# Expert rows of a product-key layer gathered as u and v halves in two phases, with 32-column products for the v sum

## What is computed

```python
def block(hb):                     # 128 tokens at a time
    ...                            # scores, two top-16 lists per head, the best 16 of their 256 sums
    idx = jnp.take_along_axis(cand_i, pos, axis=-1)            # (128 tokens, 8 heads, 16)
    gate = jax.nn.softmax(top_s, axis=-1).astype(hb.dtype)
    u = expert_u[idx]
    act = jax.nn.gelu(jnp.einsum('thkd,td->thk', u, hb), approximate=False)
    vv = expert_v[idx]
    return jnp.einsum('thk,thkd->td', gate * act, vv)
```

## Time and profile before

| | us |
|---|---|
| three runs | 3162.23, 3163.95, 3174.32 |
| median | 3163.95 |
| the profiled execution, span | 3168.1 |
| the expert stage, from `peer_clear` (948.4) to the first addition to `X` of tile 3 (2344.4) | 1396.0 |

### The profile page before, as it was taken

One profiled execution on the slowest core, in us unless ns is written; L12 is line 12 of the kernel. 1 busy time (PEld: TensorE's weight loads), 2 busy tenths in 40 slices (PEclk: granted clock), 3 DMA queues, 4 the chain that ended last, 5 costly groups with the idle time before them and its releaser, 6 DMA issues. The chain is left out here.

```text
span 3168.1 us, 23012 instructions
## 1 busy us (share of the span) xinstructions
PE 2617.8 (83%) x7588; PEld 1312.0 (41%) x7588; DVE 1722.4 (54%) x3834; ACT 320.4 (10%) x765; POOL 582.0 (18%) x516
## 2 busy tenths in 40 slices
PE   6799399889997777867777777787789978999998
PEld 4455399844452233322323323333334433444443
DVE  3644865432077677576676677555535647333304
ACT  1123121010010000100001000100010010111100
POOL 0000000000003434434434444344410000000000
PEclk9899599689998888889889898899889988999999
DMA  3201000032189999989999999999942121122210
GB/s 117 93 7 54 0 1 1 1 139 80 64 296 384 379 379 395 380 364 385 390 387 367 380 373 387 379 393 410 417 179 80 60 105 68 53 80 80 80 67 27
DMA packets 126790, 655.73 MB, mean 207 GB/s; under 512 B 9456, under 2 KB 12144, under 8 KB 60912
## 3 DMA queue, kind: packets, MB, share of 16 engines
q0 software_dynamic: 73728, 536.90, 41.9%
q1 hardware_dynamic: 52976, 117.74, 10.3%
HBM read 652.51 MB, written 2.10 MB: 207 GB/s over the span
## 5 line engine op out<-in xcount | busy, mean ns | idle before, releaser
L705 PE MATMUL PD<-AR,C 128*128 128x512 f32 x2048 | 1027.9, 661 | 349.2 <-DVE C L1511 348.9
L1654 POOL DMA_INDIRECT AR<-in_uv,C x512 | 581.8, 1136 | 1740.7 <-DVE C L1452 926.5
L1503 DVE CUSTOM_DVE_ANT_0 AR<-AR,HN 128x1024 f32<-128x1024 f32 x512 | 620.2, 1225 | 426.3 <-DMA AR<-in_uv,C 420.3
L705 PEld LDWEIGHTS PD<-AR,C 128*128 128x128 f32 x2048 | 423.7, 212 | 953.4 <-issue 494.7
L435 PE MATMUL PA<-HT,WR 128*128 128x512 f32 x736 | 327.2, 604 | 3.0 <-ACT HT L810 2.1
L435 PE MATMUL PA<-AR,WR 128*128 128x512 f32 (+1 forms) x720 | 314.1, 605 | 6.4 <-ACT AR L881 4.9
L435 PEld LDWEIGHTS PA<-HT,WR 128*128 128x128 f32 x736 | 141.9, 194 | 179.1 <-issue 175.3
L435 PEld LDWEIGHTS PA<-AR,WR 128*128 128x128 f32 (+1 forms) x720 | 138.5, 194 | 181.6 <-issue 178.7
L979 ACT ACTIVATE SC<-SC 128x2 f32<-128x2 f32 x256 | 51.9, 204 | 1276.4 <-DVE SC L1503 1276.4
L1511 DVE TENSOR_SCALAR C<-C,SC 128x128 f32<-128x128 f32 x512 | 148.6, 349 | 1.6 <-ACT SC L979 1.6
L1621 DVE TENSOR_SCALAR HT<-HN,V 128x512 f32<-128x512 f32 x44 | 24.0, 546 | 198.2 <-ACT HN L1008 198.2
(11 more groups left out here) (322 smaller groups left out, 2274.4 us busy)
## 6 DMA issues: line engine op xcount, KB each, us to landing
WR<-in_w_ada SPq DMA_DIRECT2D x12, 2048.0 KB, 7.8
WR<-in_w_in SPq DMA_DIRECT2D x11, 2048.0 KB, 7.7
WR<-in_w_up SPq DMA_DIRECT2D x11, 2048.0 KB, 7.9
WR<-in_w_down SPq DMA_DIRECT2D x5, 2048.0 KB, 7.8
WR<-in_w_pq SPq DMA_DIRECT2D x4, 2048.0 KB, 8.0
AR<-in_uv,C POOLq DMA_INDIRECT x512, 9.4
WR<-in_w_o SPq DMA_DIRECT2D x2, 2048.0 KB, 7.9
WR<-in_w_out SPq DMA_DIRECT2D x2, 2048.0 KB, 7.7
```

The source lines that it names most:

```text
L705: ins = nc.tensor.matmul(acc[half], DG[:, j, :], UV[:, j, D + 512 * half:D + 512 * half + 512], start=False, stop=False)
L1503: ttr(UV[:, j, 0:D], UV[:, j, 0:D], HN[:, t, :], 1.0, 0.0, ALU.mult, ALU.add, DOT[:, g, j % GRP:j % GRP + 1]).then_inc(s["dots"], 1)
L1654: nc.gpsimd.indirect_dma_start(UV[:, turn % RING, :], None, uv, bass.IndirectOffsetOnAxis(ap=IDX[:, t % 2, i:i + 1], axis=0),).then_inc(uv ...
```

## The change

A gathered row is now 4 KB, and the ring `ROWS` has 16 slots of 4 KB instead of 8 of 8 KB, in the same memory. A tile has two phases of 128 gathers.

In the **u phase** gather k fetches, for each token (partition), the u row of its selection k. VectorE forms 128 sums into `DOTS`. Then ScalarE does one gelu over the 128 x 128 matrix, VectorE multiplies it by the gates, TensorE transposes it, and VectorE copies it to `WT`: now a partition is a selection and a column a token.

In the **v phase** a gather fetches, for one token, the v rows of its 128 selections, one to a partition. The indices for it are the transposed index matrix `IDXT`. Four tokens q, q + 32, q + 64, q + 96 make a quad. VectorE writes for each quad four 128 x 32 matrices that are zero but for column q, which holds the token's weights (line 1502 of the changed kernel, 8 slots ahead of TensorE). TensorE multiplies each with its token's row in two halves; the four products of a half go to four different groups of 32 output partitions. The number of 512-column products stays 256 a tile, and the zero products go. `select` for the next tile now runs in the v phase, a step ahead of every fourth quad, and `layer_rows` at the end of the tile.

```diff
-RING = 8
-GRP = 2
+RING = 16
+QUADS = P // 4
+WSLOTS = 8
@@ views of the shared tile AR
-        UV = AR[:, 0:RING * 2048].rearrange("p (r n) -> p r n", r=RING)
+        ROWS = AR[:, 0:RING * D].rearrange("p (r n) -> p r n", r=RING)
+        DOTS = ar(22528, NSEL)
+        WT = ar(22656, P)
-        DG = lvl[:, 0:1024].rearrange("p (r n) -> p r n", r=RING)
+        WQ = lvl[:, 0:1024].rearrange("p (r j n) -> p r j n", r=WSLOTS, j=4)
@@ TensorE
-                acc = [bank("d"), bank("d")]
-                for half in range(2):
-                    nc.tensor.matmul(acc[half], cc("zero")[0:1, :], fours, start=True, stop=False)
-                for first, last in ((0, TURN_AT), (TURN_AT, TURNS)):
-                    if first > 0 and t > 0:
-                        turn_block("xn3", t - 1, "aa")
-                    with pe.Fori(first, last) as it:
-                        for j in range(RING):
-                            pe.wait_ge(s["diag"], it * RING + (NSEL * t + j + 1))
-                            for half in range(2):
-                                ins = nc.tensor.matmul(acc[half], DG[:, j, :],
-                                                       UV[:, j, D + 512 * half:D + 512 * half + 512],
-                                                       start=False, stop=False)
-                            ins.then_inc(s["uv_used"], 1)
-                for half in range(2):
-                    full("d", nc.tensor.matmul(acc[half], cc("zero")[0:1, :], fours, start=False,
-                                               stop=True))
+                pe.wait_ge(s["idx"], t + 1)
+                transposes("d", [SS[t][:, 0:NSEL]])
+                if t > 0:
+                    turn_block("xn3", t - 1, "aa")
+                pe.wait_ge(s["wtok"], t + 1)
+                transposes("d", [DOTS])
+                acc = [bank("d"), bank("d")]
+                for q in range(QUADS):
+                    pe.wait_ge(s["wquad"], QUADS * t + q + 1)
+                    for half in range(2):
+                        for j in range(4):
+                            i = 2 * NSEL * t + NSEL + 4 * q + j
+                            if half == 0:
+                                pe.wait_ge(row_full[i % RING], 16 * (i // RING + 1))
+                            ins = nc.tensor.matmul(acc[half][32 * j:32 * j + 32, :], WQ[:, q % WSLOTS, j, :],
+                                                   ROWS[:, i % RING, 512 * half:512 * half + 512],
+                                                   start=(q == 0), stop=(q == QUADS - 1))
+                        if q == QUADS - 1:
+                            full("d", ins)
+                    if q < QUADS - 1:
+                        ins.then_inc(s["v_used"], 1)
+                pe.drain().then_inc(s["v_used"], 1)
@@ ScalarE
                 gate_exp(t)
-                for first, last in ((0, NORM_AT), (NORM_AT, TURN_AT), (TURN_AT, TURNS)):
-                    if first == NORM_AT and t > 0:
-                        roots(ffv(t - 1))
-                    if first == TURN_AT and t > 0:
-                        turned_both(t - 1)
-                    with act.Fori(first, last) as it:
-                        for g in range(RING // GRP):
-                            act.wait_ge(s["dots"], it * RING + (NSEL * t + GRP * (g + 1)))
-                            A(GEL[:, g, :], DOT[:, g, :], ACT.Gelu).then_inc(s["gelu"], 1)
+                if t > 0:
+                    turned_both(t - 1)
+                act.wait_ge(s["u_used"], NSEL * (t + 1))
+                tell(A(DOTS, DOTS, ACT.Gelu), "gelud")
+                roots(ffv(t))
@@ VectorE (select, step 7, then the loop over tiles)
-                    link(nc.vector.tensor_copy(IDX[:, t % 2, :], acc_[0]), "idx")
+                    link(ts(IDX[:, t % 2, :], acc_[0], 2.0, None, ALU.mult), "idx")
+                b = take()
+                link(ts(IDXT, b[:, 0:P], 2.0, 1.0, ALU.mult, ALU.add), "d_free")
+                tell(dve.nop(), "idxt")
                 gates(t)
...
+                for k in range(NSEL):
+                    i = 2 * NSEL * t + k
+                    row = ROWS[:, i % RING, :]
+                    dve.wait_ge(row_full[i % RING], 16 * (i // RING + 1))
+                    tell(ttr(row, row, HN[:, t, :], 1.0, 0.0, ALU.mult, ALU.add, DOTS[:, k:k + 1]), "u_used")
+                dve.wait_ge(s["gelud"], t + 1)
+                tell(tt(DOTS, DOTS, GATE[:, t % 2, :], ALU.mult), "wtok")
+                b = take()
+                link(nc.vector.tensor_copy(WT, b[:, 0:P]), "d_free")
+                by_quad = WT.rearrange("p (j q) -> p j q", j=4)
+                for q in range(QUADS):
+                    if q % 4 == 0 and t + 1 < NT:
+                        select(t + 1, q // 4)
+                    if QUADS * t + q >= WSLOTS:
+                        dve.wait_ge(s["v_used"], QUADS * t + q - WSLOTS + 1)
+                    tell(stt(WQ[:, q % WSLOTS, :, :], cc("iota").unsqueeze(1).broadcast_to([P, 4, 32]), float(q),
+                             by_quad[:, :, q:q + 1].broadcast_to([P, 4, 32]), ALU.is_equal, ALU.mult), "wquad")
                 for half in range(2):
                     b = take()
                     xs = X[:, t, 512 * half:512 * half + 512]
                     link(tt(xs, xs, b, ALU.add), "d_free")
-            layer_rows("xn3", NT - 1, X[:, NT - 1, :], HN[:, NT - 1, :])
+                layer_rows("xn3", t, X[:, t, :], HN[:, t, :])
@@ GpSimd
+            rows = uv.rearrange("e (h d) -> (e h) d", h=2)
+            def gather(i, index):
+                if i == RING // 2:
+                    pool.wait_ge(s["peer_clear"], 1)
+                if i >= RING:
+                    half, r = divmod(i - RING, NSEL)
+                    if half % 2 == 0:
+                        pool.wait_ge(s["u_used"], NSEL * (half // 2) + r + 1)
+                    else:
+                        pool.wait_ge(s["v_used"], QUADS * (half // 2) + r // 4 + 1)
+                nc.gpsimd.indirect_dma_start(
+                    ROWS[:, i % RING, :], None, rows, bass.IndirectOffsetOnAxis(ap=index, axis=0),
+                ).then_inc(row_full[i % RING], 16)
             for t in range(NT):
                 pool.wait_ge(s["idx"], t + 1)
...
+                for k in range(NSEL):
+                    gather(2 * NSEL * t + k, IDX[:, t % 2, k:k + 1])
+                pool.wait_ge(s["idxt"], t + 1)
+                for r in range(P):
+                    token = 32 * (r % 4) + r // 4
+                    gather(2 * NSEL * t + NSEL + r, IDXT[:, token:token + 1])
```

More of the change, by code:

```diff
@@ L153, in constants @@
     put("invfreq", (np.float32(10000.0) ** (-np.arange(HALF, dtype=np.float32) / np.float32(HALF)))[None, :])
-    put("iota", np.arange(TOPK)[None, :])
+    put("iota", np.arange(32)[None, :])
     cnt = [1.0 / np.minimum(np.arange(16) + 1, w) for w in POOL]
@@ L204, in build @@
                  "ct", "x1t", "tmid", "ycomb",
-                 "topk", "idx", "dots", "geluv", "diag", "uv_used", "csil",
+                 "topk", "idx", "idxt", "u_used", "geluv", "gelud", "wtok", "wquad", "v_used", "csil",
                  "bufs", "conv", "convsq", "silu_in", "silu", "pooled", "merged",
@@ L212, in build @@
         w_sem = [ctx.enter_context(nc.semaphore(f"w_slot{i}")) for i in range(NWR)]
-        uv_full = [ctx.enter_context(nc.semaphore(f"uv_full{i}")) for i in range(RING)]
+        row_full = [ctx.enter_context(nc.semaphore(f"row_full{i}")) for i in range(RING)]
         n = {nm: 0 for nm in names}
@@ L1443, in select @@
                     link(tt(eq, tpv.unsqueeze(2).broadcast_to([P, NSEL, TOPK]),
[L1444 removed]
+                            cc("iota")[:, 0:TOPK].unsqueeze(1).broadcast_to([P, NSEL, TOPK]), ALU.is_equal))
                     for h in range(H):
@@ L1488, in _ @@
             for t in range(NT):
+                b = take()
+                link(ts(IDXT, b[:, 0:P], 2.0, 1.0, ALU.mult, ALU.add), "d_free")
+                tell(dve.nop(), "idxt")
                 gates(t)
-                cuts = (0, NORM_AT) + (SELECT_AT if t + 1 < NT else ()) + (TURNS,)
-                for first, last in zip(cuts[:-1], cuts[1:]):
-                    if first == NORM_AT and t > 0:
-                        layer_rows("xn3", t - 1, X[:, t - 1, :], HN[:, t - 1, :])
-                    if first in SELECT_AT:
-                        select(t + 1, SELECT_AT.index(first))
-                    with dve.Fori(first, last) as it:
-                        for g in range(RING // GRP + 1):
-                            if g < RING // GRP:
-                                for j in range(GRP * g, GRP * g + GRP):
-                                    dve.wait_ge(uv_full[j], it * 16 + 16 * (NSEL // RING * t + 1))
-                                    ttr(UV[:, j, 0:D], UV[:, j, 0:D], HN[:, t, :], 1.0, 0.0, ALU.mult, ALU.add,
-                                        DOT[:, g, j % GRP:j % GRP + 1]).then_inc(s["dots"], 1)
-                            if g >= 1:
```

(5 more changed lines are left out.)

25 lines of the change are left out of this document (3 added, 22 removed), and 2 rows, old and new, of the table JOBS.

## The result

| | before | after |
|---|---|---|
| median of four runs each | 3163.1 us (3160.5 to 3174.3) | 3287.6 us (3275.7 to 3299.3) |
| ratio to before, 95% interval | | 1.040 (1.036 to 1.044) |
| span of the profiled execution | 3168.1 us | 3273.7 us |
| rows' stage, 948.4 us to the first addition to `X` of tile 3 | 1396 us | 1504 us |

The change made the kernel 4.0% slower; 3125 us, 1.2% faster, was forecast. The stage was to take 1356 us and takes 1504. What follows the stage is as long as before (821 us against 824), so all of the loss lies in the stage.

What follows compares the result with a forecast made beforehand. Transfers were taken to bound the rows' stage: from 948.4, 3.9 us to the first new row, 1015 gathers x 1.32 = 1340, three dry spells x 3 = 9, last quad 3.5; 39.6 us less, so 3125 us, range 3085 to 3330.

Steps and rivals of the forecast that it cites:

- Where the gain could come from: Rows' stage: about 16 us a tile to win in three tiles, and some 9 us at each end of a tile.
- The transfers, a pitch of 1.32 us: DMA queues: a half gather costs 1.282 to 1.351 us, middle 1.32 taken; short rows bring no gain.
- Rival 2: DMA queues: half gathers carry a price of their own, pitch 1.42 us, 3226 us in all; chance 0.09.
- GpSimd, a pitch of 1.24 us: Issue of gathers: 0.94 us each with 0.30 us between, under the transfers' 1.32, as products don't stretch them.
- Rival 3: GpSimd binds: gathers keep their mean of 1.136 us, pitch 1.44 us, 3247 us in all; chance 0.05.
- VectorE, 1.15 us: u phase: products start 1.15 us apart, so 147 us a phase lies under the transfers' 169 us.
- TensorE in the v phase: Column groups overlap in pairs: 3.5 us a quad, bounds 6.9 and 1.7, under 5.3 us for its four gathers.
- Rival 1: TensorE binds the v phase, column groups not overlapping: quad 6.9 us, 3322 us in all; chance 0.24.
- The seams: Between phases: u to v leaves the engines dry about 3 us, TensorE starting some 14 us late; v to u costs nothing.
- The sum: Stage's end: terms add to 2304.8 where 2344.4 us stood, 39.6 us less, giving 3125 us for the kernel.

Runs made afterwards that it cites:

- run 6: The kernel before, with its selection for the next tile cut into 14 pieces, one ahead of each turn 1 to 14, in place of 8 steps: 3117.8 us.
- run 7: The kernel before, with tile 0's selection and gates serving all four tiles, so no selection runs beside the rows: 3095.8 us.
- run 1: The changed kernel, with VectorE's u-phase products over 64 of the 1024 columns, their sums left incomplete: 3265.9 us.
- run 13: The kernel of run 5 (tables apart), with VectorE's products narrowed to 64 of the 1024 columns: 3092.0 us.
- run 14: The kernel of run 9 (swapped halves), with VectorE's products narrowed to 64 of the 1024 columns: 3091.2 us.
- run 3: The changed kernel, with a quad's four products all going to one group of 32 output columns, the group changing every eight quads: 3444.7 us.
- run 5: The changed kernel, with u rows and v rows in two tables of adjoining 4 KB rows instead of halves of 8 KB rows (tables apart): 3164.7 us.
- run 9: The changed kernel, 8 KB rows kept, with u and v halves changed over in the rows of experts 8192 and up (swapped halves): 3187.0 us.

## Why the prediction was wrong, point by point

**Where the gain could come from: right.** That tiles 0 to 2 lose some 16 us each to the selection on VectorE is borne out by runs 6 and 7 (47 and 69 us). The pace of 2.49 us between products that it read is, by its own figures, a little faster than the 2.564 us of 409 GB/s; it went on with the latter.

**The transfers, a pitch of 1.32 us: the step that failed.** It said that a half gather costs between 1.282 and 1.351 us. Measured: 1.40 us in the queues with the table as it was (run 1), and 1.28 with tables apart or halves swapped (runs 13 and 14). So the lower bound is what half gathers cost by themselves, and the upper bound fell short because it was taken from the wrong rows. The landings of 4 KB loads and the fit over q0 and q1 are of whole rows, q0's from a gather that reads all 8 KB of each. None of them reads the same half of every row, and the change makes each gather do that. The fitted 15.3 ns a packet is 9 ns by the packets' medians. Rival 2 (1.42 us) had nearly the size, with a wrong cause: twice a price per packet. It got 0.09.

The Trainium skill (DMA: Bandwidth & Descriptors, Latency and other measured facts) has a near relation: copies whose rows lie 4 or 8 MiB apart run at about half speed, and 4 KiB of padding restores them; it calls the aliasing of memory channels an inference. The loss here is of the same kind, in another pattern: random rows, pieces that share their place within 8 KB, 365 to 373 GB/s against 400 to 409. That the cause is channels or banks is not shown here either.

**GpSimd, a pitch of 1.24 us: failed in the u phase.** The step read off one gather of 0.94 us beside a product and one of 1.48 us over the diagonals that products don't stretch gathers. In after nothing but products runs there, and gathers take up to 1.99 us; with narrow products they take 0.94 to 0.96 (runs 1 and 13). A gather is stretched or not by when the next product starts, and in the pair that was read it started 0.15 us behind the gather, among those that are never stretched (1.06 us at most). So that pair proved nothing, and the mean of 1.136 us over all 512 gathers, which the step explained away, was the number to take: the u phases have 1.13 to 1.19. The v phases, and those of tables apart, are near the forecast's 0.94 (0.94 to 0.99 in the mean). Rival 3 was thus right for half of the stage.

The Trainium skill (SBUF — State Buffer, Who interferes with whom) states that a VectorE instruction with two inputs in SBUF contends with a GpSimd instruction that reads SBUF; it also tells of a probe in which an instruction with two inputs did not stall DMA. The product has two such inputs and the gather reads its indices. By the rule the stretch was to be expected, by the probe it was not; the trace agrees with the rule in that the stretch comes and goes with the products, though six in ten gathers beside them take no more than 1.0 us.

**VectorE, 1.15 us: right.** Where rows lie ready in after, its products start 1.14 to 1.23 us apart, and over the u phases it stands 83 us for rows.

**TensorE in the v phase: right, and better than forecast.** 2.2 us a quad where 3.5 was taken; run 3 shows that without the overlap the kernel is 157 us slower than after. Rival 1's condition did not hold, and its price was short: it put the kernel without overlap at 3322 us, 158 us above before, and run 3 takes 3445. Its v phase was priced well (213 us in tile 1 of run 3, 223 priced), its u phase was not: from the first product to TensorE's start run 3 takes 199 us, some 160 were priced. That 157 and 158 look alike is chance.

**The seams: right in kind, short in size.** Dry time of 3 us a tile was forecast. TensorE starts 22, 23 and 13 us after the start of the last product in tiles 0 to 2, where 14 was taken. In tile 0 five of these microseconds are one pause within the selection (tile 1 has the like; the same step of before has none; its cause was not tried; runs 5 and 9, with the same step at the same place, don't have it and start TensorE after 13.4 us in all three tiles, so in these runs it goes with the layout):

```profile
1145.85 0.29 DVE L1392 MATCH_REPLACE8 HT<-SC,HT 128x128 f32<-128x128 f32 x1 [0.62 <-issue]
...
1150.82 1.45 DVE L1395 MAX8 SC<-HT 128x8 f32<-128x128 f32 x7 [4.69 <-remote]
```

The slowest 16 rows in a line around this seam take 1.95, 2.04 and 2.13 us each in tiles 0 to 2, against 1.42 to 1.44 behind them, some 9 us a tile (estimate). From v to u the cost was put at nothing, since VectorE would catch up at 1.15 us against 1.32. It does, but while it catches up the gathers are stretched most, as the result's section shows: in after rows 17 to 32 of a tile take 1.51 to 1.59 us each from tile 1 on, against 1.42 to 1.45 behind them, 1 to 2 us a tile; with tables apart they take 1.70 to 1.80 us, against 1.28 with narrow products.

**The sum.** 148 us lie between 1356 and 1504: 1015 gathers at about 1.45 in place of 1.32 us are 132, three seams at 9 in place of 3 us are 18. The mean pitch is the term that was mis-sized, in the u phase by GpSimd (1.44 us, with 1.40 in the queues behind it) and in the v phase by the queues. The stated range, up to 3330 us, holds the 3288 us only because it was drawn over rival 1, which did not happen. That is luck: the stage is far over the 1380 us that the forecast named as its sign of being wrong.

**What stays open.** Which part of the memory is asked for too often when all pieces share their place within 8 KB; why u gathers with swapped halves and full products still have 4.7 to 8.6 long packets and with tables apart 1.9 to 4.9, while both have next to none once the products are narrow; and how VectorE's products and the packets' times hang together.

## What to carry to other kernels

When a gather is cut in parts, ask where the parts lie in memory, not only how many bytes and packets they are: reading the same half of every row cost 9 to 11% of the rate, and a second table, or swapped halves, gave it back, the table at no price in instructions. A contention between two engines is read from the mean over a stretch in which only these two run, not from one pair of rows, and is looked for first where one of them catches up without a pause; and when two limits stand within 3% of each other (1.44 and 1.40 us), removing one shows almost nothing. Long steps of an engine that drains a ring are worth cutting finely before any rearrangement: that alone gave 1.4% here, and the rearrangement none.

## What the runs showed of the hardware that was not expected

- 128 random pieces of 4 KB move at 409 GB/s (1.28 us) when they lie anywhere, and at 365 to 373 GB/s when all lie in the same half of 8 KB rows. The median packet is 159 ns in both; in the second case three to five of a gather's 128 take over 100 ns longer.
- Four float32 products with 32 output columns each, in four column groups, overlap about three times: 2.2 us for 16 passes against 7.1 to 7.6 us in one group.
- VectorE's product over 1024 columns with both inputs in SBUF stretches a gather on GpSimd from 0.94 to as much as 1.99 us, 1.13 to 1.19 us in the mean of a u phase; the same product over 64 columns does not. A gather that starts less than 0.3 us ahead of a product is not stretched (1.06 us at most of 196).
- Of 128 packets of 8 KB, 4 to 5 take over 100 ns longer than the median in the kernel before too, and of 128 packets of 4 KB only 0.05 where tables are apart or halves swapped and the products are narrow (u phases of tiles 1 to 3).
